# A two-layer decoder trunk: order of the weight loads for values and gates, and place of the last output-weight splits

## The chip, the cores and the metric

The kernel runs on one core of one Trainium2 chip. The metric is the device time of one execution in microseconds. The kernel before takes 873.26 us (median of 3 timed runs, 872.56 to 873.67). Five engines work in parallel, each through its own list in program order: TensorE (PE, with its weight loads PEld), VectorE (DVE), ScalarE (ACT), GpSimd (POOL), and SyncE (SP), which issues nearly all DMAs. They wait for one another by semaphores.

## The reference, cut to what matters

The trunk has two layers for 1024 tokens of width 1024. The even layer (attention and a state-space branch) lies before the change and is not touched. The odd layer is:

```python
def odd_layer(x, w_in, w_gk2, b_gk, g_norm, w_out):
    h = x @ w_in
    q, k, v, gk_low, g = _split(h, ODD_SPLITS)
    o = gla_layer(q, k, v, gk_low, w_gk2, b_gk, g_norm) * jax.nn.silu(g)
    return o @ w_out
...
x = layer_norm(DEEPNORM_ALPHA * x + y, ln_g[layer], ln_b[layer])
```

The change touches how v and g (two products of 1024x1024 by 1024x1024 each) get their weights, and how w_out is made ready. `gla_layer` is chunked gated linear attention with a state carried from tile to tile.

## The kernel before, in words

**Split pairs.** Each float32 operand of a large product is held as a high part (a rounded copy, made by ACT) and a low part (operand minus high, made by DVE), and a product is three matmuls: high x high, high x low, low x high.

**Values and gates.** v and g are computed by a Strassen-like scheme with seven block products, in the order A11, A12, S3, A22, S2, S1, S4. Each product runs first for v ("v1"), then for g ("g1"), and each of these takes four slices of weights (k = 0 to 3, a slice is 128x512). That makes NVG = 56 slices, numbered n = 8 x product + 4 x (g) + k. For one slice TensorE runs 12 matmuls of 512 columns (`values_gates`, L2385). Slices 0 to 3 come from earlier buffers (`wv`); the other 52 come from DRAM pieces of 256 KB.

**Pieces and sums.** Weights land in a ring of six buffers `vg_piece`. `VG_LOADS` is the order of the loads; an entry is (kind, slice). Kinds A11, A12 and S4 are one plain piece for their slice. The others feed POOL (`block_sums`, L1145 to L1151): T3 is the difference of two pieces, the weights of product S3 (slices 16 to 23), kept in `block_sum`; T2 adds a piece to that, giving S2's weights (slice numbers 24 to 31 in the list, used in slices 32 to 39), and may run only when slice n-8 of S3 has been split; T4 subtracts that sum from a piece, in the piece's own buffer, giving A22's weights (slices 24 to 31); T1 makes those of S1 (40 to 47), after slice n-8 has been split. `VG_SUMS` is the list of the T entries, in the order of `VG_LOADS`; POOL works through it.

**The ring's rule.** SP issues the loads in the order of the list (L953). Piece number p takes buffer p mod 6, and its load waits until piece p-6 has been read (`piece_read`): for a T3, T2 or T1 piece until its sum is done; for a plain piece, and for a T4 piece, until its slice has been split. There are 60 pieces.

**The order on ACT and DVE** is written out by ticks, tick t being about the time in which TensorE works on slice t. In tick t, ACT copies the high part of slice t+2 (`vg_hi`, L1424) once TensorE has finished slice t-1 and the piece or sum is there, then makes high parts of row operands (L1431), then moves out a product of slice t-4. DVE makes the low part of slice t+2 (`vg_lo`, L1919), then row sums (`rows_sum`: S3 in ticks 0 to 3 and S1 in 8 to 11 with three operations each, S2 in 4 to 7 and S4 in 16 to 19 with two), then low parts of rows (L1926: S3 in ticks 12 to 15, S1 in 20 to 23, S2 in 26 to 29, S4 in 30 to 33), then adds a finished product from PSUM (`product_sum`, L1963), which empties its bank. TensorE claims a bank for product p+1 only when product p has left it. A slice's low part is what TensorE waits for at the slice (`vg_split`).

**Output weights.** `w_out` of the odd layer comes in four quarters. ACT scales and copies the high part (`w_out1_hi`, L1454), DVE makes the low part (`w_out1_lo`, L1913), four operations each per quarter. Three quarters are done in the ticks 36 to 56. The last quarter's load is issued after the last product.

**The stage behind it** (`gla_steps`) runs over 8 token tiles i, with these steps on every engine in the same order: kT1 i+1 and at i+1 (transposes of the keys `KS`, attention products), z1 i-3 (output product, first for i = 3, with the layer norm on DVE), yT1 i-2 (transposes of the gated output, first for i = 2), ks i (state product), o i (output of the attention). POOL makes the key tiles `KS` (L1163, L1165), the scaled queries `QS` (L1179) and, late, the last scaling and shift by `ln_gb` (L1187). SP loads `ln_gb` behind the last quarter of `w_out` (L977). z1 0 waits for all 16 splits of `w_out`.

Of the kernel before, what the change touches and what calls it, by code (L numbers as in the profile page):

```python
# [110 lines left out]
def hybrid_trunk(nc, x, x_cols, ln_g, ln_b, even_w_in, pos_cols, vec_cols, s5_rows, s5_skip, mla_w_uq,  # L111
# [28 lines left out]
    with ExitStack() as ctx:  # L140
# [227 lines left out]
        w_out0_loaded, ln_loaded = [sem(f"w_out0_loaded{s}") for s in range(2)], sem("ln_loaded")  # L368
# [200 lines left out]
        for h in range(GH + 1):  # L569
            for m in range(2 * h, 2 * h + 2 if h < GH else 0):  # L570
                plan.give(("gate", m), 6 + m % 2)
            for m in range(max(1, 2 * h - 1), min(2 * h + 1, 2 * GH)):
# [3 lines left out]
        A11, A12, S3, A22, S2, S1, S4 = range(7)  # L576
# [1 line left out]
        NVG = 56  # L578
        BLOCKS = {"A11": ((0, 0),), "A12": ((1, 0),), "S4": ((1, 1),),
                  "T3": ((1, 1), (0, 1)), "T2": ((0, 0),), "T4": ((1, 0),), "T1": ((1, 1),)}  # L580
        VG_LOADS = ([("A11", n) for n in range(4, 8)] + [("A12", n) for n in range(8, 16)]
                    + [("T3", n) for n in range(16, 20)]
                    + [pair for n in range(20, 24) for pair in (("T3", n), ("T2", n + 4))]
                    + [pair for n in range(24, 28) for pair in (("T4", n), ("T2", n + 4))]
                    + [("T4", n) for n in range(28, 32)] + [("T1", n) for n in range(40, 48)]
                    + [("S4", n) for n in range(48, 56)])
        VG_SUMS = [load for load in VG_LOADS if load[0][0] == "T"]

# [409 lines left out]
        def _(pool):  # L998
# [167 lines left out]

            keys_at_end(0)
            keys_at_end(1)
            pool.wait_ge(ln_loaded, 64)
            for i in range(NT + LAG):  # L1170
                if i + 2 < NT:
                    keys_at_end(i + 2)
                if i == 0:
                    plan.filled(pool, ("g1", S4, 3))
                if 1 <= i < NT:
                    if i >= 3:
                        plan.filled(pool, ("o1", i - 2, 1))
                    for c, decays in enumerate((ends[:, :, 2 * i - 1:2 * i], two_ends[:, :, i:i + 1])):
                        step(pool.tensor_tensor(QS[:, i % 2, :, c * GC:(c + 1) * GC],  # L1179
                                                QD[:, :, i * P + c * GC:i * P + (c + 1) * GC],  # L1180
                                                decays.to_broadcast([P, GH, GC]), ALU.mult), qs_set if c else None)
                if LAG <= i < NT + LAG - 1:
                    j = i - LAG
                    pool.wait_ge(centred, NT + j + 1)

                    z = SG[:, j, :]
                    step(pool.tensor_tensor(z, z, ln_gb[:, 0, :], ALU.mult))  # L1187
                    step(pool.tensor_tensor(z, z, ln_gb[:, 1, :], ALU.add), y_set)
# [3 lines left out]
        def _(act):  # L1192
# [276 lines left out]
            for what, i in gla_steps():  # L1469
                if what == "kT1":  # L1470
                    plan.filled(act, ("kT1", i))
                    if i >= 2:
                        plan.filled(act, ("ks", i - 2, 1))
                    step.frees(act.activation(kTok[:, i % 2, :, :], bank("kT1", i).rearrange("p (h d) -> p h d", h=GH),
                                              ACT.Copy), ("kT1", i))
                elif what == "o":
                    for hp in range(2):
                        plan.filled(act, ("o1", i, hp))
                        for j in range(2):
                            step(act.activation(sq[:, :], bank("o1", i, hp)[:, j * GDV:(j + 1) * GDV], ACT.Square,  # L1480
                                                accum_out=stat[:, 32 + 2 * hp + j:33 + 2 * hp + j]))
                            step.settle()
                    r = 36 + 4 * (i % 2)
                    step(act.activation(stat[:, r:r + 4], stat[:, 32:36], ACT.Sqrt, bias=eps[:, 1:2], scale=1.0 / GDV),
                         ms_set)
                    if i == 0:
                        for j in range(4):
                            w_out1_hi(3, j)
                elif what == "yT1":
                    for half in range(2):  # L1490
                        plan.filled(act, ("yT1", i, half))
                        if half == 0:
                            y1t_free(act, i)
                        step(act.activation(Y1T[y1t_slot(i)][0][:, 4 * half:4 * half + 4, :],
                                            bank("yT1", i, half).rearrange("p (k t) -> p k t", k=4), ACT.Copy),
                             yT1_hi_set)
                elif what == "z1":
                    act.wait_ge(var_set, NT + i + 1)
                    step(act.activation(stat[:, 20:21], stat[:, 1:2], ACT.Sqrt, bias=eps[:, 0:1]), root_set)
# [3 lines left out]
        def _(vec):  # L1503
# [263 lines left out]
            for k in range(4):  # L1767
                m, n = k // 2, k % 2
# [49 lines left out]
            for what, n in attention_steps():  # L1818
# [24 lines left out]
                elif what == "av" and heads[n][1] == H - 1:  # L1843

                    i = heads[n][0]
# [139 lines left out]
            for what, i in gla_steps():  # L1985
# [6 lines left out]
                elif what == "ks":  # L1992
                    for hp in range(2):
                        plan.filled(vec, ("ks", i, hp))
                        for j in range(2):
                            h = 2 * hp + j
                            src = bank("ks", i, hp)[:, j * GDV:(j + 1) * GDV]
                            if i == 0:
                                ins = vec.tensor_copy(state[:, 0, h, :], src)
                            else:  # L2000
                                ins = vec.scalar_tensor_tensor(state[:, i % 2, h, :], state[:, (i - 1) % 2, h, :],
                                                               two_ends[:, h, i:i + 1], src, ALU.mult, ALU.add)
                            if j:
                                step.frees(ins, ("ks", i, hp))
                            else:
                                step(ins)
                    step.settle()
                elif what == "o":
                    vec.wait_ge(ms_set, i + 1)
                    serial(vec.reciprocal(stat[:, 44:48], stat[:, 36 + 4 * (i % 2):40 + 4 * (i % 2)]))  # L2010
                    for hp in range(2):
                        for j in range(2):
                            h = 2 * hp + j
                            s = slice(h * GDV, (h + 1) * GDV)
                            ins = vec.scalar_tensor_tensor(SG[:, i, s], bank("o1", i, hp)[:, j * GDV:(j + 1) * GDV],
                                                           stat[:, 44 + h:45 + h], SG[:, i, s], ALU.mult, ALU.mult)
                            if j:
                                step.frees(ins, ("o1", i, hp))
                            else:
                                step(ins)  # L2020
                    if i == 0:
                        for j in range(4):
                            w_out1_lo(3, j)
                elif what == "yT1":
                    for half in range(2):
                        vec.wait_ge(yT1_hi_set, 2 * i + half + 1)
                        ks = slice(4 * half, 4 * half + 4)
                        hi, lo = Y1T[y1t_slot(i)]
                        step.frees(vec.tensor_tensor(lo[:, ks, :],
                                                     bank("yT1", i, half).rearrange("p (k t) -> p k t", k=4),  # L2030
                                                     hi[:, ks, :].bitcast(F32), ALU.subtract), ("yT1", i, half))
                elif what == "z1":
                    vec.wait_ge(x1_back[i % 4], 16 * (i // 4 + 1))
                    layer_norm(SG[:, i, :], V1[:, i, :], "z1", i, NT + i)
                    if i == NT - 1:
                        vec.wait_ge(ln_loaded, 64)
                        step(vec.scalar_tensor_tensor(SG[:, i, :], SG[:, i, :], stat[:, 0:1], ln_gb[:, 0, :],
                                                      ALU.subtract, ALU.mult))
                        vec.wait_ge(root_set, NT + i + 1)
                        serial(vec.reciprocal(stat[:, 21:22], stat[:, 20:21]))  # L2040
                        for n in range(2):
                            z = SG[:, i, n * 512:(n + 1) * 512]
                            step(vec.scalar_tensor_tensor(z, z, stat[:, 21:22], ln_gb[:, 1, n * 512:(n + 1) * 512],
                                                          ALU.mult, ALU.add), y_last_set)
# [446 lines left out]
```

## Time and profile before

| what | value |
|---|---|
| median of the timed runs | 873.26 us |
| the profiled execution, its own time | 871.63 us |
| its span | 869.90 us |
| TensorE busy | 825.6 us, 95% |
| DVE, ACT, POOL busy | 589.7, 361.5, 271.4 us |
| granted TensorE clock, mean | 0.998 |

Time is read from the span; the profiled execution is 1.7 us longer than it, for what lies outside the first and last instruction. Busy shares say which engine is full on average; where an engine waits, and for whom, is read from the stretches, the waits and the timelines. The loop over the 56 slices starts at 549.5 us and ends near 711 us; the stage behind it runs to the end.

### The profile page before, as it was taken

To read this page: it belongs to the slowest core of one execution; us is meant where nothing else is said; L and a number is where in the kernel's file an instruction comes from. 1 tells how busy PE (TensorE), PEld (TensorE's weight loads), DVE (VectorE), ACT (ScalarE), POOL (GpSimd) and SP (SyncE) were. 2 spreads that over 40 slices of the span, in tenths; PEclk is the share of its full clock that TensorE was granted. 3 is DMA by queue.
4 is the path that set the end of the run, shared out by engine and by line. 5 is a ranking of instruction groups with operands and counts; after the bars stand their busy time and mean duration, and the time that the engine had idled before them with its cause. 6 is when DMAs were issued, how large, how long until landed. Compare 5 with 4: busy or idle time off the path is not lost.

```text
span 869.9 us, 12216 instructions
## 1 busy us (share of the span) xinstructions
PE 825.6 (95%) x4192; PEld 670.0 (77%) x4192; DVE 589.7 (68%) x960; ACT 361.5 (42%) x689; POOL 271.4 (31%) x281
## 2 busy tenths in 40 slices
PE   7998999999998999989999999999799999999996
PEld 5898878667786766678877888887678888888885
DVE  5898698757765777748871453688886677554553
ACT  6341512874325666832232663155234446111220
POOL 2000000526214342308866440017642013332242
PEclk9999999999999999999999999999999999999999
DMA  9101163410000300052224110337333222111111
GB/s 325 54 20 31 49 121 80 71 28 2 1 2 0 122 1 2 1 170 97 98 98 121 49 48 1 109 92 242 106 129 122 74 97 74 44 54 49 49 49 73
DMA packets 40829, 64.20 MB, mean 74 GB/s; under 512 B 8272, under 2 KB 21840, under 8 KB 40752
## 3 DMA queue, kind: packets, MB, share of 16 engines
q1 hardware_dynamic: 40768, 63.42, 24.1%
q8 instruction: 34, 0.56, 0.3%
q14 instruction: 27, 0.22, 0.1%
HBM read 52.33 MB, written 9.44 MB: 71 GB/s over the span
## 4 chain that ended last, share of the span: by engine, by line
PE 46%; DVE 8%; DMA 1%; POOL 1%; ACT 1%; issue 1%; SPq 0%; DVEq 0%; ACTq 0%; POOLq 0%
PE psum L2052 30%; PE psum L2385 14%; PE psum L2061 2%; DVE vg_lo L1919 1%; DVE x_lo_raw L1951 1%; DVE x_hi_raw L1950 1%; DMA ln_gb<-ln_b_dram 1%; DVE zn L1535 1%; DVE stat L1529 1%; DVE zn L1526 1%; DVE x1T_lo L1926 1%; DVE gs_lo L1809 1%; DMA vg_piece<-odd_w_in_dram 1%; DVE x1T_lo L1878 0%; PE psum L2298 0%
## 5 line engine op out<-in xcount | busy, mean ns | idle before, releaser
L2385 PE MATMUL psum<-vg_hi,x1T_hi 128*128 128x512 f32 x208 | 81.6, 393 | 7.0 <-DVE vg_lo L1919 5.7
L2385 PE MATMUL psum<-vg_lo,x1T_hi 128*128 128x512 f32 x208 | 81.0, 389 | 0.0
L2385 PE MATMUL psum<-vg_hi,x1T_lo 128*128 128x512 f32 x208 | 81.0, 389 | 0.0
L2144 PE MATMUL psum<-kT,qTt 96*128 96x512 f32 (+3 forms) x192 | 73.1, 491 | 1.2 <-DVE YT L762 1.2
L1751 DVE TENSOR_REDUCE negmax<-psum 128x1 f32<-128x640 f32 (+5 forms) x64 | 48.5, 758 | 26.3 <-PE psum L2148 24.8
L1305 ACT ACTIVATE prob<-psum,negmax 128x640 f32<-128x640 f32 (+5 forms) x64 | 47.4, 741 | 15.7 <-DVE negmax L1751 7.1
L2385 PEld LDWEIGHTS psum<-vg_hi,x1T_hi 128*128 128x128 f32 x208 | 39.0, 188 | 17.5 <-DVE vg_lo L1919 7.4
L2052 PE MATMUL psum<-w_out_hi,Y1T_hi 128*128 128x512 f32 x128 | 50.5, 395 | 0.0
L2052 PE MATMUL psum<-x1T_hi,wqk_hi 128*128 128x512 f32 x128 | 50.0, 391 | 0.0
L2052 PE MATMUL psum<-w_out_hi,Y1T_lo 128*128 128x512 f32 x128 | 49.9, 390 | 0.0
L2052 PE MATMUL psum<-w_out_lo,Y1T_hi 128*128 128x512 f32 x128 | 49.9, 390 | 0.0
L2052 PE MATMUL psum<-x1T_hi,wqk_lo 128*128 128x512 f32 x128 | 49.9, 390 | 0.0
L2052 PE MATMUL psum<-x1T_lo,wqk_hi 128*128 128x512 f32 x128 | 49.8, 389 | 0.0
L2061 PE MATMUL psum<-ident,prob 128*128 128x128 f32 x288 | 43.1, 277 | 6.0 <-ACT prob L1305 6.0
L1355 ACT ACTIVATE probT_hi<-psum 128x512 fp32r<-128x512 f32 x64 | 33.2, 518 | 36.9 <-PE psum L2061 15.2
L1836 DVE TENSOR_TENSOR probT_lo<-psum,probT_hi 128x512 fp32r<-128x512 f32 x64 | 37.8, 591 | 14.5 <-ACT probT_hi L1355 12.8
L2385 PEld LDWEIGHTS psum<-vg_hi,x1T_lo 128*128 128x128 f32 x208 | 39.0, 188 | 8.2
L2385 PEld LDWEIGHTS psum<-vg_lo,x1T_hi 128*128 128x128 f32 x208 | 39.0, 188 | 8.0
L2144 PEld LDWEIGHTS psum<-kT,qTt 96*128 96x128 f32 x192 | 32.2, 190 | 16.8 <-issue 16.7
L1526 DVE SCALAR_TENSOR_TENSOR SG<-V,psum 128x512 f32<-128x512 f32 x16 | 11.0, 688 | 49.3 <-PE psum L2052 49.3
L1032 POOL MEMSET TT<- 128x2048 f32 x1 | 1.8, 1810 | 134.6 <-PE psum L2061 134.6
L2061 PEld LDWEIGHTS psum<-ident,prob 128*128 128x128 f32 x288 | 32.9, 147 | 13.8 <-ACT prob L1305 12.0
(419 smaller groups left out, 2238.1 us busy)
## 6 DMA issues: line engine op xcount, KB each, us to landing
vg_piece<-odd_w_in_dram SPq DMA_DIRECT2D x60, 256.0 KB, 3.3
x_res<-x_dram SPq DMA_DIRECT2D x8, 512.0 KB, 4.2
wqk_raw<-odd_w_in_dram SPq DMA_DIRECT2D x8, 512.0 KB, 5.1
x_scratch<-zn SPq DMA_DIRECT2D x8, 512.0 KB, 2.9
w_out_raw<-odd_w_out_dram SPq DMA_DIRECT2D x4, 1024.0 KB, 5.0
V<-x_scratch SPq DMA_DIRECT2D x8, 512.0 KB, 4.3
xT_raw<-x_cols_dram SPq DMA_DIRECT2D x7, 512.0 KB, 8.5
out_dram<-SG SPq DMA_DIRECT2D x7, 512.0 KB, 2.9
```

The costliest lines, as they stand in the source:

```text
L1305: step.frees(act.activation(prob[:, place:place + (i + 1) * P], src, ACT.Exp, bias=negmax[:, n % 4:n % 4 + 1], accum_out=rsum[:, i % 4, h: ...
L1355: step(act.activation(hi, source, ACT.Copy), prob_hi_set)
L1526: step.frees(vec.scalar_tensor_tensor(zt[:, s], res[:, s], ALPHA, bank(job, i, n), ALU.mult, ALU.add), (job, i, n))
L1529: serial(vec.bn_stats(stat[:, 48 + 6 * n:54 + 6 * n], zt[:, s]))
L1535: step(vec.tensor_scalar(zt, zt, stat[:, 0:1], stat[:, 21:22], ALU.subtract, ALU.mult), centred)
L1751: step(vec.tensor_reduce(negmax[:, n % 4:n % 4 + 1], scores(n)[0], AX_X, ALU.max, negate=True), max_set)
L1809: step(vec.tensor_tensor(gs5_lo[:, :, cols], gs5[:, :, cols], mix_hi[i % 2][:, 4:6, :].bitcast(F32), ALU.subtract), mix_split)
L1836: step.frees(vec.tensor_tensor(lo, source, hi.bitcast(F32), ALU.subtract), ("pt", number))
L2052: mm = pe.matmul(out, lhsT, rhs, start=(k == 0), stop=(k == len(pairs) - 1))
L2061: mm = pe.transpose(bank(*job)[0:rows, k * P:k * P + cols], block_in, identity[0:cols, 0:cols])
L2144: mm = pe.matmul(psum[:, slot + part, 0:c1 - c0], qTt[:, i % 2, h, :], kT[:, h, c0:c1], start=True, stop=not diag, skip_group_check=diag)
L2385: mm = pe.matmul(bank(*job), lhsT, rhs, start=(k == 0 and j == 0 and product not in ADDS_TO), stop=(k == 3 and j == len(pairs) - 1), skip_ ...
```

## The change

Three things are moved; no operation is added or removed.

1. In `VG_LOADS`, T3's pairs now alternate with A12's slices, one pair behind each, and T2 and T4 alternate from slice 24 to 31 with equal slice numbers. `VG_SUMS` follows, so POOL's order changes likewise.
2. POOL's wait for `ln_gb` stands directly ahead of the first use in place of ahead of the loop over the tiles.
3. The last quarter of `w_out` is split in two steps on ACT and DVE: parts 0 and 1 after o 1, parts 2 and 3 after yT1 0, in place of all four after o 0.

```diff
-        VG_LOADS = ([("A11", n) for n in range(4, 8)] + [("A12", n) for n in range(8, 16)]
-                    + [("T3", n) for n in range(16, 20)]
-                    + [pair for n in range(20, 24) for pair in (("T3", n), ("T2", n + 4))]
-                    + [pair for n in range(24, 28) for pair in (("T4", n), ("T2", n + 4))]
-                    + [("T4", n) for n in range(28, 32)] + [("T1", n) for n in range(40, 48)]
+        VG_LOADS = ([("A11", n) for n in range(4, 8)]
+                    + [pair for n in range(8, 16) for pair in (("A12", n), ("T3", n + 8))]
+                    + [pair for n in range(24, 32) for pair in (("T2", n), ("T4", n))]
+                    + [("T1", n) for n in range(40, 48)]
                     + [("S4", n) for n in range(48, 56)])
...
             keys_at_end(0)
             keys_at_end(1)
-            pool.wait_ge(ln_loaded, 64)
             for i in range(NT + LAG):
...
                 if LAG <= i < NT + LAG - 1:
                     j = i - LAG
+                    if j == 0:
+                        pool.wait_ge(ln_loaded, 64)
                     pool.wait_ge(centred, NT + j + 1)
...
                     step(act.activation(stat[:, r:r + 4], stat[:, 32:36], ACT.Sqrt, bias=eps[:, 1:2], scale=1.0 / GDV),
                          ms_set)
-                    if i == 0:
-                        for j in range(4):
-                            w_out1_hi(3, j)
+                    for j in range(2 if i == 1 else 0):
+                        w_out1_hi(3, j)
                 elif what == "yT1":
...
                              yT1_hi_set)
+                    for j in range(2, 4 if i == 0 else 2):
+                        w_out1_hi(3, j)
...
                                 step.frees(ins, ("o1", i, hp))
                             else:
                                 step(ins)
-                    if i == 0:
-                        for j in range(4):
-                            w_out1_lo(3, j)
+                    for j in range(2 if i == 1 else 0):
+                        w_out1_lo(3, j)
                 elif what == "yT1":
...
                                                      hi[:, ks, :].bitcast(F32), ALU.subtract), ("yT1", i, half))
+                    for j in range(2, 4 if i == 0 else 2):
+                        w_out1_lo(3, j)
```

## Rows read from the trace of the kernel before

**Rows 1.** Page, engines: busy us (share of the span) and instructions.

```profile
PE 825.6 (95%) x4192; PEld 670.0 (77%) x4192; DVE 589.7 (68%) x960; ACT 361.5 (42%) x689; POOL 271.4 (31%) x281
```

**Rows 2.** Stretches: us, each engine's busy us (instructions), clock, DMA share, GB/s.

```profile
594.00:620.00 26.00, 20.27 (x86) 15.46 (x85) 25.42 (x18) 10.41 (x16) 23.03 (x15) 1.00 0.51 155
620.00:640.00 20.00, 18.69 (x81) 14.84 (x80) 16.71 (x23) 7.59 (x12) 8.75 (x6) 1.00 0.45 133
640.00:711.00 71.00, 71.00 (x317) 58.79 (x317) 49.64 (x71) 30.84 (x47) 14.93 (x12) 1.00 0.26 90
```

**Rows 3.** Chain that ended last, in order of time: start us, us, what.

```profile
549.52 43.53 PE psum L2385 x192
...
711.72 6.66 DMA ln_gb<-ln_b_dram
...
718.51 0.62 POOL KS L1163
...
719.64 0.66 PE psum L2061 x4
```

**Rows 4.** TensorE's waits, 545 to 740 us: total us, times, longest.

```profile
PE psum L2385 <- DVE vg_lo L1919: 5.7, 4, 2.1
PE psum L2061 <- POOL KS L1165: 1.1, 1, 1.1
...
PE psum L2385 <- DVE SG L1963: 0.6, 1, 0.6
```

**Rows 5.** ACT's timeline: start us, us, operation, [idle before <- what ended it].

```profile
563.21 0.63 ACT L1424 ACTIVATE vg_hi<-vg_piece 128x512 fp32r<-128x512 f32 x1 [4.15 <-PE psum L2385]
...
640.08 0.63 ACT L1424 ACTIVATE vg_hi<-v_block_sum 128x512 fp32r<-128x512 f32 x1 [1.45 <-PE psum L2385]
...
667.28 0.63 ACT L1424 ACTIVATE vg_hi<-v_block_sum 128x512 fp32r<-128x512 f32 x1 [1.33 <-PE psum L2385]
```

**Rows 6.** DVE's timeline, same columns.

```profile
563.94 0.69 DVE L1919 TENSOR_TENSOR vg_lo<-vg_piece,vg_hi 128x512 fp32r<-128x512 f32 x1 [0.84 <-ACT vg_hi L1424]
564.67 0.69 DVE L1940 TENSOR_TENSOR SG<-x1T_hi,V 128x512 f32<-128x512 f32 x1
...
594.99 1.67 DVE L1950 TENSOR_TENSOR x_hi_raw<-x1T_hi,SG 128x512 f32<-128x512 f32 x1
596.69 1.67 DVE L1951 TENSOR_TENSOR x_lo_raw<-x_hi_raw,x1T_lo 128x512 f32<-128x512 f32 x1
...
617.00 0.69 DVE L1963 TENSOR_TENSOR V<-V,psum 128x512 f32<-128x512 f32 x1
```

**Rows 7.** POOL's timeline, same columns.

```profile
578.46 1.29 POOL L1145 TENSOR_TENSOR v_block_sum<-vg_piece,vg_piece 128x512 f32<-128x512 f32 x1 [58.18 <-DMA vg_piece<-odd_w_in_dram]
...
596.19 1.62 POOL L1147 TENSOR_TENSOR v_block_sum<-v_block_sum,vg_piece 128x512 f32<-128x512 f32 x1
...
625.10 1.29 POOL L1149 TENSOR_TENSOR vg_piece<-vg_piece,v_block_sum 128x512 f32<-128x512 f32 x1 [6.98 <-DMA vg_piece<-odd_w_in_dram]
```

**Rows 8.** Loads of vg_piece: all, those from 588 to 600, from 640 to 700.

```profile
DMA to landing us min/median/max: 2.6/3.3/6.4
...
DMA to landing us min/median/max: 2.7/3.6/4.6
...
DMA to landing us min/median/max: 2.6/5.3/6.4
```

**Rows 9.** Timelines of DVE and TensorE in the stage behind the loop.

```profile
713.00 0.73 DVE L1990 COPY_PREDICATED att<-tile_tri,psum 128x512 f32<-128x512 int32 x1 [0.59 <-PE psum L2052]
716.69 1.89 PE L2052 MATMUL psum<-V,att 128*128 128x256 f32 x8
...
724.13 3.49 DVE L1913 SCALAR_TENSOR_TENSOR w_out_lo<-w_out_raw,vecs,w_out_hi 128x512 fp32r<-128x512 f32 x4
...
737.65 0.48 PE L2052 MATMUL psum<-w_out_hi,Y1T_hi 128*128 128x512 f32 x1
```

## The prediction

> **What bounds the kernel now.** The page first: TensorE is busy for 95% of the span [rows 1], so a change elsewhere can only pay where TensorE waits. The table by stretches of the values-and-gates loop (56 slices of weights, 12 matmuls each) shows where that is: TensorE is full from 640 us, and ahead of that, from 594 on, it is busy 20.27 of 26.00 and 18.69 of 20.00 us, while DVE is busy 25.42 of 26 and POOL 23.03 of 26 [rows 2]. The chain of waits has the loop start at 549.52 us [rows 3], and the waits of TensorE name DVE's split of the weights (`vg_lo`, L1919) as what it waited for, four times [rows 4].
>
> Busy time of a pipelined engine understates the loss, so I take it from the cadence. ACT may copy slice n (`vg_hi`, L1424) when TensorE has finished slice n-3, so undisturbed copies mark TensorE's pace. From 640.08 (slice 32) to 667.28 (slice 42) are ten slices: 2.72 us each. From 563.21 (slice 7) to 640.08 are 25 slices: 76.87 us, where 25 x 2.72 = 68.00 [rows 5]. **TensorE loses 8.87 us here.**
>
> Why, is in DVE's and POOL's timelines. Alone, a DVE operation on SBUF tiles takes 0.69 us, one every 0.73 (563.94, 564.67). Beside POOL's block sums it takes 1.67, one every 1.70; one that reads PSUM (L1963) keeps its 0.69 [rows 6]. POOL's sum takes 1.29 alone and 1.62 beside DVE [rows 7]. They take turns: each sum costs a busy DVE 1.70 - 0.73 = 0.97 us. The Trainium skill, "SBUF — State Buffer", on the port pair shared by VectorE and GpSimd, states an exclusive lock for the whole instruction. By that a pair would need 0.69 + 1.29 = 1.98 us and a sum would cost DVE 1.25; the rows show 1.70, so I count with 0.97.
>
> The cushion: when DVE keeps up, slice 7 is split at 563.94 + 0.69 = 564.63 and TensorE needs it at 549.52 + 7 x 2.72 = 568.56: 3.9 us [rows 3, 6]. From 593.86 to 618.7 DVE works through 16 operations, 11.6 us alone, with 14 sums of an unbroken row of POOL work beside them, 13.6 us. 593.86 + 25.2 = 619.1 for the split of slice 23, due at 549.52 + 62.56 = 612.1: 7.0 of the 8.87 us. The other 1.9 come behind it: POOL waits 6.98 us for the piece of a T4 sum at 625.10 [rows 7], and one wait is for the emptying of a PSUM bank (L1963) [rows 4].
>
> **The new load order.** No load, sum or operation is added or removed; 60 pieces, 32 sums. What changes is when a sum can start, and that is set by the ring of six pieces: the load of piece p waits until piece p-6 was read. Before, the first T3 pair is pieces 12 and 13 of the ring, so the first sum waits 58.18 us and starts at 578.46 [rows 7]; 23 more follow, up to 634. After, piece 4+3i is A12's slice 8+i and pieces 5+3i, 6+3i are T3's pair for slice 16+i. The first pair waits only for the split of slice 4, the second for that of slice 7, the next for A12's slices two back, so about one T3 sum falls in each slice. I wrote the queues out by these rules, with 0.73 and 0.97 us for DVE, 0.63 for ACT, 2.72 per slice and 3.5 us from issue to landing; the same writing-out for the old order gives 8.7 us of loss against the 8.87 of the trace.
>
> T3 sums then start near 560, 568, 572, 576, 579, 583, 587 and 591, and T2/T4 run from 593 to 605. DVE has the row differences of S1 there (ticks 8 to 11: 3 operations and a split each, 2.9 us for 2.72). Step by step:
> - To slice 14: from the end of slice 10's split at 572.9, 12 row operations and 4 splits are 16 x 0.727 = 11.6; five sums meet them, 4.85. Slice 14 is split at 589.35, due at 549.52 + 38.08 = 587.6. **Loss 1.8 us**, 1.15 of it at slice 14 itself.
> - To slice 20: 14 operations (4 parts of S3's rows, 6 splits, 4 sums for S4) are 10.2; eight sums (the last T3, T2 and T4 to 605), 7.8. Split at 607.3, due at 603.9 + 1.8 = 605.7. **Loss 1.6 us.**
> - Then the ring stops POOL for some 14 us: T4's fourth piece needs the place of its first, which is read only at slice 24's split, near 616. DVE recovers. That load lands near 619.5 and its sum is done by 621, slice 27 being due at 626.4: hidden. Behind it T2 and T4 sums alternate, two per slice (2.6 us of 2.72 alone). DVE stands waiting for slice 29's T4 sum while its next entry is the emptying of S3's last bank, which TensorE wants in slice 28. The nearest row is the 0.6 us bank wait [rows 4]; written out it is 0.6 to 1.5. **Loss 0.9 us.**
>
> Together 4.3 us in place of 8.87: 4.6 saved. (By the whole-instruction lock of the Trainium skill's page, each of the 13 sums above would cost 0.28 us more, and 3.6 of these 4.6 would be gone; the rows of 1.67 and 1.70 speak against that price, and I give it no share.) What I am least sure of is the landing time. The loop's median is 3.3 us, in the burst of 588 to 600 it is 3.6 and at most 4.6 [rows 8]. With 2.9 my writing-out loses 3.9, with 3.8 it loses 4.8, with 4.4 it loses 6.2, so the saving runs from 5.0 to 2.7; the old order moves little with it (8.0 to 9.3).
>
> **POOL's wait for ln_gb moved.** Before, POOL waits for both rows of `ln_gb` (landed at 718.4, after the 6.66 us of the last DMA) ahead of its third key tile; TensorE's transpose of it starts at 719.64 [rows 3]. TensorE's operations before it, 8 matmuls from 716.69 at 0.215 us, end at 718.4 [rows 9]: a hole of 1.2 us (1.1 in the waits [rows 4], up to 1.5 counting the weight load). After, POOL makes the tile from about 713, when tile 0's product is complete (DVE takes that bank at 713.00 [rows 9]), and waits for `ln_gb` only ahead of the first use, 30 us later (POOL's order: behind it QS for tile 3 and its own L1187). Who follows as late: the next o product wants QS (two POOL operations behind the key tiles, there by 717) and the copies of the state, which DVE makes while TensorE runs the o product before; the next transposes want the bank that DVE empties at 724.1 and TensorE reaches it at 725.9. None binds. **1.2 us saved.**
>
> **Last quarter of w_out in two steps.** The same 4 ACT and 4 DVE operations, 3.49 us on DVE from 724.13 [rows 9], placed later. They leave the kTok copy and tile 2's `att` earlier, which is cover, not gain: TensorE has no hole after 719.64 in this stage. The new bound: output 0 waits for all 16 splits. In DVE's order, from 724.13 with the durations of that stage and ACT's sums of squares ahead: o1's scaling ends 729.7, two splits 731.5, `att` 732.2, two Y1T parts 733.7, two splits **735.45**; TensorE wants them at 737.65 - 1.2 = 736.4. Margin 0.95 us. Cost nothing; if ACT or DVE slips by 2 us it takes 1 us back. No effect below zero: nothing else of TensorE's waits for them.
>
> **Sum.** 4.6 + 1.2 = 5.8 us. The profiled execution took 871.63 us (span 869.90) and becomes 865.8; it lay 1.6 under the median of the three timed runs, 873.26, which becomes **867.5**.
>
> **Rivals.**
> - *Nearly no stall left* (863.2 to 865.5). Sums that fall beside PSUM-reading or waiting DVE cost nothing; before slice 20 DVE reads no PSUM, though, and ticks 8 to 11 are over full even without POOL. All of it gone would be 8.87 + 1.2: 863.2. Chance 0.12.
> - *Most of the contention only moves, since loads are slow* (869.5 to 871.5): three pieces per slice are 768 KB in 2.72 us, landing times of 4.4 to 5 us, loss of 6.2 to 8. Speaks for it: six loads in a row landed after up to 4.6 [rows 8]. Chance 0.18.
> - *Slower*: A12's slice n can now be loaded only when slice n-2 is split and the T3 loads ahead of it on SP are issued. Two slices, 5.44 us, must hold landing + 1.4 for ACT and DVE + 0.97 for a sum + 0.4 of queue. That decides from about 5.6 us of landing. At 6.4, the longest seen, a round takes 9.2, loses 3.8, four rounds 15 less the cushion of 3.9, with some 3 behind: 14 in place of 8.87 + 1.2, so 877. Against: 5.3 to 6.4 stand only in the stretch with 1 MB loads ahead on the queue [rows 8]. Chance 0.05.
> - *No difference*: landing near 5.3, or the order doesn't bring the sums forward since something else holds POOL; only the 1.2 us or less stays. 872 to 873.5. Chance 0.08.
>
> The forecast (866 to 869.5) has 0.57. The range 864.3 to 871.2 leaves out about half of the first rival, some of the second and the last two, 2 in 10. A change of 0.2%, 1.75 us, is what a measurement can tell from none. Faster by that: 0.57 + 0.12 + nearly all of 0.18, 0.86; same 0.09; slower 0.05.
>
> **What the profile will show.** T3 sums from about 560 us, one per slice, DVE operations of 1.67 us scattered among ticks 8 to 13 rather than in one block; copies of slices 16 and 17 about 0.6 and 1.8 us late by the 2.72 cadence; no POOL work from about 606 to 619; TensorE's loop some 4.6 us shorter; no wait of the third KS tile for `ln_gb`; first z1 matmul with no wait for `w_out_lo`. I am wrong if landing in 565 to 590 has a median above 4.4 us, if the loss sits in slices 24 to 31, or if z1 waits.

## The result, and the profile after

The changed kernel takes 867.48 us (median of 4 runs, 866.95 to 868.64) against 873.40 (4 runs, 872.56 to 873.67): a ratio of 0.9938, 95% interval 0.9922 to 0.9954, 4.0 to 6.8 us less. The forecast was 867.5. Its profiled execution took 867.0 us with a span of 865.3, 4.6 us under the span of before. So the median fell on the forecast, but the two profiles differ by 4.6 where the sum said 5.8; what follows takes that sum apart.

The stretches of the loop, as in [rows 2] (us, then busy us and instructions of PE, PEld, DVE, ACT, POOL, then clock, DMA share, GB/s):

```profile
594.00:620.00 26.00, 24.56 (x107) 19.68 (x106) 25.11 (x27) 11.99 (x19) 11.51 (x7) 1.00 0.19 53
620.00:640.00 20.00, 19.11 (x84) 15.51 (x83) 16.91 (x19) 8.63 (x15) 14.11 (x10) 1.00 0.46 145
```

From 594 to 620 us TensorE is busy 24.56 us in place of 20.27, DVE runs 27 instructions in its 25 busy us in place of 18, and POOL is busy 11.5 us in place of 23. TensorE's waits from 545 to 740 us, beside [rows 4]: there is no wait for POOL's key tile any more, and of the two waits for a PSUM bank before (0.6 us in [rows 4], and 0.7 us of `V` at the same line) one is left, of 0.9 us (now L1964).

```profile
PE psum L2387 <- DVE vg_lo L1920: 2.8, 3, 1.3
PE psum L2387 <- DVE SG L1964: 0.9, 1, 0.9
```

ACT's copies of the high parts give the cadence, as in [rows 5]; these are slices 7, 15, 17 and 32:

```profile
563.50 0.64 ACT L1424 ACTIVATE vg_hi<-vg_piece 128x512 fp32r<-128x512 f32 x1 [4.15 <-PE psum L2387]
...
590.03 0.63 ACT L1424 ACTIVATE vg_hi<-vg_piece 128x512 fp32r<-128x512 f32 x1 [4.07 <-DMA vg_piece<-odd_w_in_dram]
...
592.82 0.63 ACT L1424 ACTIVATE vg_hi<-v_block_sum 128x512 fp32r<-128x512 f32 x1 [0.23 <-PE psum L2387]
...
636.88 0.63 ACT L1424 ACTIVATE vg_hi<-v_block_sum 128x512 fp32r<-128x512 f32 x1 [0.32 <-PE psum L2387]
```

25 slices took 636.88 - 563.50 = 73.38 us; less 68.00 that is **5.38 us of loss, in place of 8.87**. Ten slices from 7 to 17 took 29.32, 2.12 too many. ACT stood 1.78, 1.97 and 4.07 us for the pieces of slices 13, 14 and 15 to land; in the old order no copy from slice 7 to 32 waited for its piece.

POOL's timeline, beside [rows 7]: the first T3 sum, one of those between, the last T2 sum before the pause, and the T4 sum that ends it.

```profile
559.17 1.75 POOL L1144 TENSOR_TENSOR v_block_sum<-vg_piece,vg_piece 128x512 f32<-128x512 f32 x1 [38.49 <-DMA vg_piece<-odd_w_in_dram]
...
586.05 1.57 POOL L1144 TENSOR_TENSOR g_block_sum<-vg_piece,vg_piece 128x512 f32<-128x512 f32 x1 [2.30 <-DMA vg_piece<-odd_w_in_dram]
...
605.03 1.70 POOL L1146 TENSOR_TENSOR v_block_sum<-v_block_sum,vg_piece 128x512 f32<-128x512 f32 x1 [0.72 <-DVE vg_lo L1920]
620.93 1.29 POOL L1148 TENSOR_TENSOR vg_piece<-vg_piece,v_block_sum 128x512 f32<-128x512 f32 x1 [14.20 <-DMA vg_piece<-odd_w_in_dram]
```

DVE's timeline around slice 14, beside [rows 6]: a row operation that met the sum of 586.05 takes 1.66 us, the split 0.69, and the split of slice 14 ends at 589.62. TensorE's next lines show the slice starting on it, after 0.86 us of idling.

```profile
586.51 1.66 DVE L1947 TENSOR_TENSOR x_lo_raw<-x1T_lo 128x512 f32<-128x512 f32 x1
...
588.93 0.69 DVE L1920 TENSOR_TENSOR vg_lo<-vg_piece,vg_hi 128x512 fp32r<-128x512 f32 x1
```

```profile
589.68 0.50 PE L2387 MATMUL psum<-vg_hi,x1T_hi 128*128 128x512 f32 x1 [0.86 <-DVE vg_lo L1920]
590.02 0.40 PE L2387 MATMUL psum<-vg_lo,x1T_hi 128*128 128x512 f32 x1
```

Behind the loop, beside [rows 9]: the third key transpose follows the o product at once (715.21), and z1 starts at 732.99, DVE's last two splits of `w_out` having ended at 732.40.

```profile
713.49 1.89 PE L2054 MATMUL psum<-V,att 128*128 128x256 f32 x8
715.21 0.60 PE L2063 MATMUL psum<-ident,KS 128*128 128x128 f32 x4
...
732.99 0.48 PE L2054 MATMUL psum<-w_out_hi,Y1T_hi 128*128 128x512 f32 x1
```

```profile
730.86 1.54 DVE L1914 SCALAR_TENSOR_TENSOR w_out_lo<-w_out_raw,vecs,w_out_hi 128x512 fp32r<-128x512 f32 x2
```

### The profile page after: what moved, and what is told of

Read it like the earlier page. It is cut to its first block, busy times and chain, and to the rows that moved or that the text cites. A ratio compares the mean times of both kernels' runs of the same rounds, so it can differ in the third digit from the quotient of the medians.

```text
span 865.3 us, 12216 instructions
## 1 busy us (share of the span) xinstructions
PE 826.4 (96%) x4192; PEld 671.9 (78%) x4192; DVE 591.5 (68%) x960; ACT 361.2 (42%) x689; POOL 272.2 (31%) x281
## 4 chain that ended last, share of the span: by engine, by line
PE 44%; DVE 10%; POOL 1%; ACT 1%; DMA 1%; issue 1%; DVEq 0%; SPq 0%; ACTq 0%; POOLq 0%
PE psum L2054 31%; PE psum L2387 11%; PE psum L2063 2%; DVE vg_lo L1920 2%; DVE x1T_lo L1927 1%; DMA vg_piece<-odd_w_in_dram 1%; DVE zn L1536 1%; DVE stat L1530 1%; DVE zn L1527 1%; DVE x_lo_raw L1952 1%; DVE gs_lo L1810 1%; DVE x1T_lo L1879 0%; DVE x_lo_raw L1948 0%; DVE x_hi_raw L1951 0%; DVE x_lo_raw L1947 0%
## 5 line engine op out<-in xcount | busy, mean ns | idle before, releaser
L1187 POOL TENSOR_TENSOR SG<-SG,ln_gb 128x1024 f32<-128x1024 f32 x7 | 16.6, 2375 | 85.5 <-DVE SG L1536 85.5
```

## The experiments

Two lengths are read from every profile: the **loop loss** (ACT's copies of slices 7 to 55 less 48 x 2.72 us) and the **stage**, from the first key transpose to the first z1 matmul. The first transpose stands at 710.56 us before and 707.35 after, so the stage is 27.09 and 25.64 us. Both are of one profiled execution per kernel. "Before" in each line of timed runs is the kernel before on the same chip.

| kernel | loop loss | stage | span | ratio to before, 95% interval |
|---|---|---|---|---|
| before | 8.87 | 27.09 | 869.9 | |
| changed | 5.38 | 25.64 | 865.3 | 0.9938, 0.9922 to 0.9954 |
| changed, again (e9) | 5.07 | 25.63 | 863.4 | 0.9929, 0.9911 to 0.9948 |
| load order only (e1) | 4.81 | 26.97 | 865.5 | 0.9952, 0.9934 to 0.9971 |
| ln_gb wait only (e2) | 9.20 | 26.72 | 871.4 | 0.9994, 0.9978 to 1.0011 |
| w_out in two steps only (e3) | 9.34 | 26.81 | 871.0 | 1.0005, 0.9989 to 1.0021 |
| new order, no sums (e4) | 0.00 | 25.64 | 860.6 | one execution |
| old order, no sums (e5) | 0.00 | 26.98 | 862.5 | one execution |
| one more DMA per T3 (e6) | 5.21 | 25.63 | 865.8 | one execution |
| three more DMAs per T3 (e11) | 10.20 | 25.63 | 869.3 | one execution |
| bank first (e7) | 4.21 | 25.63 | 864.2 | 0.9926, 0.9901 to 0.9951 |
| bank first, S4 later (e8) | 1.98 | 25.63 | 862.2 | 0.9927, 0.9903 to 0.9951 |
| rows spread (e10) | 0.31 | 25.64 | 860.6 | 0.9869, 0.9845 to 0.9893 |
| rows spread, old order (e12) | 6.33 | 25.64 | 867.2 | one execution |

The spans carry what lies before the loop too (its start moved between about 548 and 551 us from run to run), which is why the two lengths are used to tell kernels apart.

The loop loss holds one thing more than waits. In three of these executions the granted TensorE clock was half (1.2 in place of 2.4 GHz) for 3.4 us in the loop, each time behind waits of TensorE: e2 from 618.2 us, e11 from 595.6, e12 from 622.0. Two stretches, of e2 and of e12, with the clock third from the end:

```profile
618.10:621.30 3.20, 3.20 (x9) 2.48 (x8) 3.06 (x5) 0.00 (x0) 1.61 (x2) 0.51 0.00 0
```

```profile
622.10:625.50 3.40, 3.40 (x10) 2.66 (x9) 3.30 (x4) 0.19 (x1) 1.55 (x2) 0.51 0.69 216
```

The matmuls there start every 0.43 us in place of 0.23, which adds up to 1.6 us in each of the three. No other kernel of the table shows it in the loop. Without it e2 would stand at 7.6 us (one short wait of the old order, at slice 23, is gone there, since DVE caught up meanwhile), e11 at 8.6 and e12 at 4.7.

**e1, the load order alone.** Only `VG_LOADS` as in the change's first hunk.

> Only the new order of VG_LOADS; the wait for ln_gb and the last quarter of w_out stay as before. Theory (POOL's sums cost a busy DVE 0.97 us each, and the new order spreads them): the loop gives back what it gave in the changed kernel, 8.87 - 5.38 = 3.5 us, TensorE's hole ahead of the third key transpose stays near 1.2 us, span near 866.4, time some 3.5 us under before. Rival (the three edits help one another, or the gain of the timed runs, 5.9 us, comes from outside the loop): the loop's loss is above 7 us, or the time falls by under 2 us.

The loss is 4.81 us, the stage 26.97: the loop's gain comes from the order alone, 0.9952. The rival is out.

**e2, POOL's wait alone.**

```diff
             keys_at_end(1)
-            pool.wait_ge(ln_loaded, 64)
...
+                    if j == 0:
+                        pool.wait_ge(ln_loaded, 64)
```

> Only POOL's wait for ln_gb moved. Theory: the loop keeps its loss near 8.9 us; from the first key transpose to the first z1 matmul 27.1 us becomes 25.6 to 25.9, time 1.2 to 1.45 us under before. Rival (the hole was covered by the last quarter of w_out, whose splits then become the thing z1 or the first yT1 waits for, since all eight stay ahead of kTok and att): the stretch shrinks by under 0.5 us and TensorE shows a wait for DVE's att or w_out_lo.

The rival was nearer. The stage shrinks by 0.37 us only. TensorE's waits in this kernel between 705 and 745 us:

```profile
PE psum L2053 <- DVE SG L2016: 0.3, 1, 0.3
PE psum L2053 <- DVE state L2002: 0.2, 1, 0.2
```

The key tile is ready, TensorE runs on, and stands 11 us later at DVE (at 730.98 and 733.39): the four splits of `w_out` (3.12 us from 725.91) are ahead of tile 2's `att`, the state and the scaling of tile 1, which empties the banks of the next o product.

**e3, the last quarter in two steps alone.** The change's last hunks, on ACT and DVE.

> Only the last quarter of w_out in two steps; the wait for ln_gb and the load order as before. Theory: cover only, nothing changes: the stretch from the first key transpose to the first z1 matmul stays at 27.1 us within 0.1, loop loss near 8.9, time equal to before within 0.5 us. Rival: the 0.85 us margin of the first yT1 was in truth a wait and the stretch shrinks by 0.2 or more.

The stage is 26.81, 0.28 shorter; the time is the same (1.0005). Here TensorE keeps its hole ahead of the third transpose (1.0 us in the waits) and has no other. The stage can be cut in two at the third key transpose. e1 and e5 have the stage's code as before:

| kernel | first to third transpose | third transpose to z1 |
|---|---|---|
| before | 9.08 | 18.01 |
| e1, e5 | 8.97, 8.98 | 18.00, 18.00 |
| e2, wait edit alone | 7.86 | 18.86 |
| e3, w_out edit alone | 8.97 | 17.84 |
| changed | 7.86 | 17.78 |

The wait edit takes its 1.1 to 1.2 us from the first part in any case, and without the other edit 0.86 of it is lost again in the second. The w_out edit alone takes some 0.16 us from the second part; the other 0.11 of its 0.28 is in the first part, where e1 and e5 have it without the edit. So the rival's 0.2 or more came only in part from this edit. **Neither edit gives the 1.45 us alone.**

**e4 and e5, no sums.** POOL's 32 sums become fills with zeros; the weights of S3, S2, S1 and A22 are left out. Loads, waits and DVE's work stay.

```diff
-                if what == "T3":
-                    step(pool.tensor_tensor(total, pieces[0], pieces[1], ALU.subtract), vg_pool_sum)
...
+                step(pool.memset(pieces[0] if what == "T4" else total, 0.0), vg_pool_sum)
```

> The changed kernel, but each of POOL's 32 sums is replaced by filling its target with zeros, so the weights of the products S3, S2, S1 and A22 are left out; loads, waits, order and all of DVE's work stay. Theory (the loss is DVE being held by POOL's reads): DVE's row operations stay at 0.69 us, the loop's loss falls from 5.4 us to under 1, span near 860.5. Rival (loads land late and the queue of pieces is the bound): the loss stays above 3 us, with ACT waiting for pieces of slices 13 to 15 as now and TensorE behind it.

> The kernel before, with each of POOL's 32 sums replaced by filling its target with zeros (the weights of S3, S2, S1 and A22 are left out). Theory: the loop's loss falls from 8.87 us to under 1, so that both orders run the same loop once POOL no longer reads beside DVE. Rival (the old order is slow by itself: late loads for T3 and T4): 3 us or more stay, in slices 20 to 28.

In both orders the loss is 0.00 us. The groups of POOL and DVE in the new order's loop (line, engine, operation, count, busy us, mean ns, idle before):

```profile
L1143 POOL MEMSET v_block_sum<- 128x512 f32 x12 | 6.3, 527 | 72.6 <-DMA vg_piece<-odd_w_in_dram 52.4 <-DVE vg_lo L1913 20.2
...
L1940 DVE TENSOR_TENSOR x_lo_raw<-x1T_lo 128x512 f32<-128x512 f32 x4 | 2.8, 693 | 0.1
```

The row operations of S1, some of which took 1.66 us beside the sums, take 693 ns on average. POOL was also shorter by this edit (0.53 us in place of 1.29), but it is DVE's time that went back to 0.69, and no sum or load was late enough to matter in either order. So the whole loss of the loop, before and after, hangs on POOL's sums; at these landing times loads alone cost nothing.

**e6 and e11, more traffic.** One, and three, more DMAs of 256 KB, DRAM to DRAM, ahead of each T3 load.

```diff
                 base = {"v1": 2 * GKW, "g1": c_gk + GR}[name]
+                if what == "T3":
+                    sp.dma_start(extra_rows[n - 16, :, :], w_in1[k * P:(k + 1) * P, base:base + 512]).then_inc(extra_done, 16)
```

> The changed kernel with one more DMA of 256 KB, DRAM to DRAM, issued by SP ahead of each of the eight T3 loads: four pieces in place of three per slice, nothing else. It prices the landing time, the term I was least sure of. Theory (landing matters only once a round of two slices is over 5.44 us): the median landing between 575 and 594 us goes from 3.5 to 4.5 us or more and the loop's loss from 5.4 to between 7 and 12, all of the rise in slices 12 to 16. Rival (landing is hidden as long as DVE is the bound): the loss stays within 0.5 us of 5.4.

> The changed kernel with three more DMAs of 256 KB, DRAM to DRAM, ahead of each T3 load: six pieces per slice. With one more the landing rose by 0.6 to 0.9 us and the loop lost no more. Theory (landing decides only once a round of two slices, 5.44 us, no longer holds it, from about 5.6 us): landing of 6 us or more, slices 11 to 15 late by several us, loop loss 9 us or more. Rival (loads are hidden here in any case): loss under 6 us.

Landing of the pieces issued between 575 and 594 us, in the changed kernel, in e6 and in e11:

```profile
DMA to landing us min/median/max: 2.7/3.5/4.6
```

```profile
DMA to landing us min/median/max: 2.6/4.1/5.1
```

```profile
DMA to landing us min/median/max: 4.3/6.5/7.0
```

With a median of 4.1 us the loss is 5.21, no more than without: my theory for e6 fell (7 to 12 us), its rival held. With 6.5 us it is 10.20, of which 1.6 is the stretch at half clock. ACT's copy of slice 11 is 1.7 us late, that of slice 14 is 6.9. TensorE waits from slice 12 on (0.68 us for a split at 582.38, then 1.98 at 586.72 for a bank that ACT moves out only behind a copy whose piece was late). Landing decides somewhere between. Why it costs nothing at 4.1 us is argued only: either a late piece stands behind a DVE that is late itself, or the 3.9 us cushion takes it up. e10 below, where DVE is no longer late, speaks for the cushion: copies of slices 13 to 15 up to 1.5 us late there cost next to nothing.

**e7, the bank first.** In each tick, DVE's `product_sum` ahead of its split.

```diff
+                if tick >= 4:
+                    product, name, t = vg_slice(tick - 4)
+                    product_sum(name, product, t)
                 if 4 <= tick + 2 < NVG:
                     vg_low(tick + 2)
...
-                if tick >= 4:
-                    product, name, t = vg_slice(tick - 4)
-                    product_sum(name, product, t)
```

> The changed kernel, with DVE's addition of a finished product (which empties the PSUM bank) put ahead of the split of the slice in each tick, in place of last. Theory (TensorE's wait in slice 28 is for S3's bank, behind a DVE that waits for a T4 sum): the 0.9 us wait of TensorE for L1964 goes, the loop's loss falls from 5.4 to 4.2 to 4.6, time 0.8 to 1.2 us under the changed kernel. Rival (the T4 sums themselves are late): the wait moves to the split of slices 28 to 31 and the loss stays.

The loss is 4.21 us, as the theory had it, and the wait for the bank is gone. The waits for `vg_lo` are those of the changed kernel: 2.8 us in 3 waits, the longest 1.3.

The T4 sums stay late (the copy of slice 31 is 7.2 us behind the cadence), but the split has the cushion for that; the bank had not.

**e8, S4's rows later.** As e7, with S4's row operations in ticks 20 to 23, in POOL's pause, and S1's low parts in 34 to 37.

> As the run with the bank first, and the eight row operations for S4 are moved from ticks 16 to 19 to ticks 20 to 23, where POOL stands still for 14 us, with the low parts of S1's rows moved from ticks 20 to 23 to 34 to 37 (needed at slice 40). Theory (DVE's backlog up to slice 20 is work plus sums): the loss of 2.1 us in slices 14 to 20 goes, the 2.1 us of slices 13 and 14 stays, the loop's loss is 2.0 to 2.8 us, span near 862.5. Rival (late loads are what holds slices 13 to 20): the loss stays above 4 us.

The loss is 1.98 us, all of it in slices 13 and 14: the theory held. Its timed ratio, 0.9927, doesn't separate it from e7; the profile does.

**e9, the changed kernel again.**

> The changed kernel as it is, once more beside the kernel before, for the size of the gain. By the sum of the two stretches (3.5 us in the loop, 1.45 behind it) the gain is 4.6 to 5.0 us; by the first timed runs it was 5.9. Theory (the traces hold the whole gain): the ratio is 0.9940 to 0.9950. Rival (the timed runs gained more than the profiled ones): 0.993 or less.

0.9929, 0.9911 to 0.9948: the point value is the rival's, and the interval reaches into both. See below.

**e10, rows spread.** As e8, with S1's row operations in ticks 8, 10, 11 and 18, and ACT's high parts of them in ticks 20 to 23 in place of 18 to 21. The rest of e8's edit isn't shown.

```diff
-                for first, product in ((0, S3), (4, S2), (8, S1), (16, S4)):
-                    if first <= tick < first + 4:
+                for ticks, product in ((range(0, 4), S3), (range(4, 8), S2), ((8, 10, 11, 18), S1), (range(20, 24), S4)):
+                    if tick in ticks:
```

> The changed kernel with the bank emptied first in each tick, S4's row operations in ticks 20 to 23, S1's low parts in 34 to 37, and S1's row operations in ticks 8, 10, 11 and 18 in place of 8 to 11 (ACT's high parts of S1 in 20 to 23). Theory (DVE's own work plus 0.97 us per sum, held under the pace of TensorE with the 3.9 us cushion): nothing of the loop's loss is left, 0 to 0.6 us, span near 860.5, as with the sums left out; 9 to 12 us under before, 5 under the changed kernel. Rival (late landing of slices 13 to 15 stands behind DVE and comes out once DVE is no longer the bound): 1.5 to 3 us of loss in slices 13 to 16.

0.31 us of loss. All 32 sums are there, and the stretches show TensorE full through the place of the old hole, with DVE and POOL as busy as ever:

```profile
575.00:594.00 19.00, 19.00 (x85) 15.53 (x84) 18.39 (x19) 10.35 (x18) 8.83 (x7) 1.00 0.77 250
594.00:620.00 26.00, 26.00 (x116) 21.53 (x115) 24.46 (x27) 13.81 (x21) 12.05 (x8) 1.00 0.18 52
```

Its span is that of e4 without the sums, 860.6 us. The time is 860.61 us (median of 6, 859.98 to 865.79) against 873.08: ratio 0.9869, 0.9845 to 0.9893. That is 12.5 us under before, a little more than the 9 to 12 expected, and 5.6 under the changed kernel (e9) on the same chip.

**e12, rows spread in the old load order.**

> As the run with the rows spread, but the loads and sums in the order of the kernel before. It tells whether the new load order is still needed once DVE's work is laid out better. Theory: the old order bunches 14 sums in a row against TensorE's need, 4.5 to 6 us of loss, in slices 20 to 26. Rival (the row operations were the whole matter, the load order none): under 1 us.

6.33 us of loss, in slices 21 to 25, where 14 sums still follow one another from 594.81 to 618.44 with 0.7 us of pause at most. 1.6 us of it is the stretch at half clock, so that 4.7 us of waits are left, against 8.87 before and 0.31 with both. Both parts are needed: the order spreads POOL's sums, the ticks spread DVE's work.

## Why the prediction was right, and where only the total was

**What bounds, and the mechanism: right.** The loss lies in slices 13 to 28 and is DVE held up by POOL's sums; e4 and e5 take the sums away and 5.38 and 8.87 us become 0.00. The price of 0.97 us fits: the operation at 586.51 takes 1.66.

**The times of the sums: right.** Forecast 560, 568, 572, 576, 579, 583, 587, 591; the trace has 559.2, 567.9, 572.3, 575.4, 578.8, 582.3, 586.1, 591.4. T2 and T4 run from 594 to 607, then POOL stands for 14.20 us; forecast 593 to 605 and some 14.

**Loss to slice 14: forecast 1.8, start of the slice 1.78 late** (589.68 against 549.82 + 38.08), copies 2.12 late. **To slice 20: forecast 1.6, measured 2.07** (the copy of slice 23 is 4.19 late). **The bank in slice 28: forecast 0.9, measured 1.19.** By the copies each term is 0.3 to 0.5 too small, and 4.3 became 5.38. **This sum is the step that was off**; it made the saving 4.6 in place of 3.49.

Most of the gap is what follows a wait. I had counted to the end of the split. The first matmul starts 0.05 us later, and the next 0.34 behind it in place of 0.23: some 0.16 us for each of five waits (585.80, 589.68, 604.92, 608.07 and 633.09), 0.8 of the 1.08 us. A part is landing: before the split of slice 15, at 590.77, DVE stood 0.42 us for the late copy; in e1 and e9 it didn't, and their loss is 4.81 and 5.07. What stays open is the old order. It has six such waits, yet the same writing-out gave 8.7 against 8.87. Like with like the forecast would have been 8.7 - 4.3 = 4.4 us, so that only 0.2 of the error is the unequal comparison of a measured 8.87 with a written-out 4.3.

The list of waits understates the loss too: it has 0.86 us for slice 14, where two steps from 588.43 to 590.02 took 1.59 in place of 0.45, a loss of 1.13. A wait is counted from the end of a matmul that is drawn 0.39 long, though the next would have started 0.23 behind it.

Over all kernels with the old order and full sums the loss is 8.87, 9.20 and 9.34 (9.20 with half a clock in it), with the new order 5.38, 4.81 and 5.07: a saving of 4.05 us on the means, 4.0 without e2.

**The landing time: the wrong thing to fear.** I gave it the width of the range (2.9 us for a loss of 3.9, 4.4 for 6.2). Copies did wait for pieces (slices 13 to 15, up to 4.07 us), as the slower rival says, but e6 with 4.1 us loses nothing more. The copy of slice 16, forecast 0.6 us late, was 3.4 late behind that of slice 15, but DVE didn't have to wait for it. That rival's mechanism is real and its price was too high: at 6.4 us of landing I had 14 us of loss and 877, e11 at 6.5 us has 10.20 (8.6 at full clock) and 871.06, in one execution, still not slower than before.

**POOL's wait: 1.2 forecast, and the hole gave 1.22; the stage gave 1.45.** The first part of the stage went from 9.08 to 7.86 us, as forecast. The other 0.23 us came behind it (18.01 to 17.78), where I had put the two steps of `w_out` at nothing; e3 has 0.16 of it. "Cover, not gain" was right in the main, but the cover had no price: e2 shows that without it 0.86 of the 1.22 us is lost again. TensorE had no hole after 719.64 because the hole at 718.4 had let DVE catch up. The margin before z1, forecast 0.95, was 0.59.

**The sum.** 3.49 + 1.45 = 4.9 us between the two profiles' stretches; the spans say 4.6, since the loop started 0.30 later. That lies outside the change: in the changed kernel's profile the granted clock was half from 272.8 to 276.2 us, in the even layer. The 200 matmuls around it took 34.43 us, and 33.29 both before and in e9, where the clock was full. Up to there the changed kernel's execution had been 0.7 us ahead. The timed runs say 5.9 and 6.8 us (873.40 - 867.48; 873.08 - 866.25), with intervals that begin at 4.0 and 4.5. Means over the profiles, 4.05 in the loop and 1.4 behind it, are 5.4 and lie within. So the forecast of 5.8 is right for the timed runs.

Whether the 0.5 to 1.4 us above the traces' sum is more than scatter stays open, but the runs point at the clock. In the runs of e9 the mean granted clock is 0.9955 for the changed kernel and 0.9927 for before, and among the 11 of before the time falls by some 0.65 us for each 0.001 of it. By that slope, an estimate, the clock is 1.8 of the 6.8 us. That the old order's stalls bring half clock on more often fits e2 and e12, but before and e3 have the same stalls in their profiles without it, so it is not shown.

That 867.5 met 867.48 is luck to a tenth of a per cent: the loop's term was 0.5 to 1.1 too large, the stage's 0.25 too small.

**The range and the rivals.** "Nearly no stall left" needed the rows moved as well, as e10 did. The lock over the whole instruction would have put the two stalls up to slice 20 at 3.6 us more; they came 0.8 above the count with 0.97.

## What to carry to other kernels

When two engines take turns at something, add up both queues against the pace of the engine that they feed, tick by tick, with the cushion; moving one queue helps only as far as the other leaves room, and here the better layout of DVE's rows was worth nearly as much again as the change (5.6 us against 6.8). A wait costs more than its idle time, so measure it by cadence, and price what follows a wait when you write queues out. Where no wait shows, a wait ahead may be covering one: try each edit alone before calling one of them free. And look at the granted clock of each stretch before two loss figures are compared.

## What the runs showed of the hardware

- GpSimd filling a 128x512 float32 tile (0.53 us) beside DVE's operations with two SBUF inputs costs DVE nothing (693 ns on average); its sums with two SBUF inputs cost DVE 0.97 us each. The Trainium skill, "SBUF — State Buffer", on the shared port pair, has this: with two SBUF inputs DVE contends only with a GpSimd operation that reads SBUF. The runs agree.
- A landing time 0.6 us longer in the median, with four pieces per slice in place of three, cost a kernel with DVE as its bound nothing; 3.0 us longer cost 4.8 us, 1.6 of it at half clock.
- The same kernel's profiled executions differ by up to 1.9 us in span (865.3 and 863.4): 0.3 of it in the loop, 1.1 by the 3.4 us at half clock from 272.8 us.
- In the loop the granted clock fell to half in e2, e11 and e12, each time behind a row of waits of TensorE, the last of 2.04, 1.94 and 1.82 us, and cost 1.6 us each time. The kernel before, with waits of 1.28, 2.01 and 2.05 us, kept the full clock in its profile. The mean clock of such an execution still reads 0.992 to 0.996.
